# Grouped-query stage: four tiles projected abreast, sums and rotations dealt out anew, the last rotation cut into three steps

## The reference, cut to what matters

```python
def gqa_axial_mixer(hn, w_q, w_kv, q_gain, k_gain, w_o, cos_r, sin_r, cos_c, sin_c):
    q = (hn @ w_q).reshape(b, s, GQA_HEADS, GQA_HEAD_DIM).transpose(0, 2, 1, 3)      # 16 heads of 64
    kv = (hn @ w_kv).reshape(b, s, 2, GQA_KV_HEADS, GQA_HEAD_DIM)                    # 4 key/value heads
    k, v = kv[:, :, 0].transpose(0, 2, 1, 3), kv[:, :, 1].transpose(0, 2, 1, 3)
    q, k = rmsnorm(q, q_gain), rmsnorm(k, k_gain)                                    # over each head's 64
    def axial(t):
        return jnp.concatenate([apply_rope(t[..., :half], cos_r, sin_r),
                                apply_rope(t[..., half:], cos_c, sin_c)], axis=-1)
    o = blocked_attention(axial(q), axial(k), v, GQA_HEAD_DIM ** -0.5)
    return o.transpose(0, 2, 1, 3).reshape(b, s, GQA_HEADS * GQA_HEAD_DIM) @ w_o
```

## Time and profile before

| | |
|---|---|
| median of 3 runs | 1137.16 us (1133.55 to 1137.99) |
| the profiled execution | 1132.8 us, of which the profiler's span is 1130.9 us |
| PE busy | 1098.0 us, 97% of the span |
| DVE, ACT, POOL busy | 837.4, 619.0, 40.1 us |
| granted TensorE clock | 0.996 of full speed on average |
| the stage from its first matmul to its last output | 835.29 to 911.07 us of the span |

### The profile page before, as it was taken

One profiled execution on the slowest core, in us unless ns is written; L12 is line 12 of the kernel. 1 busy time (PEld: TensorE's weight loads), 2 busy tenths in 40 slices (PEclk: granted clock), 3 DMA queues, 4 the chain that ended last, 5 costly groups with the idle time before them and its releaser, 6 DMA issues.

```text
span 1130.9 us, 20116 instructions
## 1 busy us (share of the span) xinstructions
PE 1098.0 (97%) x7645; PEld 971.9 (86%) x7645; DVE 837.4 (74%) x1275; ACT 619.0 (55%) x1112; POOL 40.1 (4%) x42
## 2 busy tenths in 40 slices
PE   5999999999999999999999999999999899999997
PEld 5997779999899999999876889999988688888886
DVE  5698873665788878875467588788787867878875
ACT  6753446565545545573465555455465855545544
POOL 2000000010100000010000100000010001000000
PEclk9999999999999999999999999999999999999999
DMA  9551223343657657465320366656677055657651
GB/s 298 165 187 39 76 76 100 124 152 104 202 160 214 184 153 219 136 219 154 127 65 1 113 181 191 197 171 189 195 143 175 9 150 168 177 160 220 185 160 65
DMA packets 218591, 169.69 MB, mean 150 GB/s; under 512 B 20859, under 2 KB 208290, under 8 KB 218402
## 3 DMA queue, kind: packets, MB, share of 16 engines
q1 hardware_dynamic: 217106, 164.43, 49.6%
q0 software_dynamic: 912, 4.00, 1.1%
q10 hardware_dynamic: 512, 0.40, 0.1%
HBM read 167.76 MB, written 1.05 MB: 149 GB/s over the span
## 4 chain that ended last, share of the span: by engine, by line
PE 86%; DVE 5%; ACT 5%; SPq 1%; issue 1%; DMA 1%; POOLq 0%; POOL 0%; DVEq 0%; ACTq 0%
PE bank L2542 20%; PE bank L2161 18%; PE bank L2090 11%; PE bank L2092 10%; PE bank L2091 10%; PE bank L2544 10%; PE bank L2155 2%; PE bank L2156 2%; PE bank L2157 2%; DVE wlo L1427 1%; DVE arena L1420 1%; ACT arena L1370 1%; DVE wlo L1837 1%; SPq L702 1%; DMA arena<-in_ssm_lam_im_dram 1%
## 5 line engine op out<-in xcount | busy, mean ns | idle before, releaser
L2542 PE MATMUL bank<-mem_pair,whi 128*128 128x512 f32 x1056 | 375.8, 399 | 0.7 <-DVE xT L1758 0.7
L2544 PE MATMUL bank<-mem_pair,wlo 128*128 128x256 f32 x1056 | 296.7, 281 | 0.0
L2542 PEld LDWEIGHTS bank<-mem_pair,whi 128*128 128x128 f32 x1056 | 198.6, 188 | 47.5 <-issue 0.9
L2090 PE MATMUL bank<-act_hi,whi 128*128 128x256 f32 (+1 forms) x744 | 215.8, 290 | 2.3 <-DVE act_lo L1459 1.5
L1837 DVE TENSOR_TENSOR wlo<-raw,whi 128x1024 fp32r<-128x1024 f32 x177 | 208.9, 1221 | 5.3 <-ACT whi L1207 1.6
L2091 PE MATMUL bank<-act_lo,whi 128*128 128x256 f32 (+1 forms) x744 | 212.2, 285 | 0.0
L2092 PE MATMUL bank<-act_hi,wlo 128*128 128x256 f32 (+1 forms) x744 | 212.0, 285 | 0.0
L1427 DVE TENSOR_TENSOR wlo<-raw,whi 128x1024 fp32r<-128x1024 f32 (+3 forms) x137 | 162.0, 1224 | 65.6 <-ACT whi L783 64.5
L2544 PEld LDWEIGHTS bank<-mem_pair,wlo 128*128 128x128 f32 x1056 | 199.7, 189 | 0.8
L1207 ACT ACTIVATE whi<-raw 128x1024 fp32r<-128x1024 f32 x180 | 179.7, 1045 | 0.3 <-PE bank L2161 0.3
L1227 ACT ACTIVATE arena<-arena 128x256 f32<-128x256 f32 x66 | 27.6, 418 | 249.4 <-DVE arena L1420 249.4
(11 more groups left out here) (237 smaller groups left out, 1418.9 us busy)
## 6 DMA issues: line engine op xcount, KB each, us to landing
raw<-in_ffn_w_in_dram SPq DMA_DIRECT2D x132, 512.0 KB, 5.2
raw<-in_ffn_w_out_dram SPq DMA_DIRECT2D x33, 1024.0 KB, 5.0
raw<-in_w_in_ab_dram SPq DMA_DIRECT2D x11, 1024.0 KB, 6.2
raw<-in_w_in_dram SPq DMA_DIRECT2D x9, 1024.0 KB, 7.6
raw<-in_xa_wk_dram SPq DMA_DIRECT2D x4, 1024.0 KB, 5.4
raw<-in_xa_wv_dram SPq DMA_DIRECT2D x4, 1024.0 KB, 5.2
raw<-in_w_out_dram SPq DMA_DIRECT2D x4, 1024.0 KB, 5.0
raw<-in_xa_wq_dram SPq DMA_DIRECT2D x4, 1024.0 KB, 5.0
```

The lines of the kernel that those rows point to most:

```text
L2090: pe.matmul(dst, w[0], a[0], start=start, stop=False, **kw)
L2542: pe.matmul(b[:].rearrange("p (h t) -> p h t", h=2), w[0][:, k, g, :], mem_pair[:, :, k, :], start=k == 0, stop=False, skip_group_check=True)
L2544: last = pe.matmul(b[:, 0:T], w[1][:, k, g, :], mem_hi[:, k, :], start=False, stop=k == KC - 1, skip_group_check=True)
```

## The change

Three things change. First, gq0 and gq1 join the key tiles in `project_abreast`: four tiles abreast instead of two, and then gq2 to gq7 one by one. Second, the hooks are dealt out over six tiles instead of eight; gq2, gq4 and gq6 carry two each, the others one. The sum of squares of the stream goes to bank 7 instead of 5, since bank 5 now belongs to a tile in progress (gq2). Third, `g_rotate(4)` is cut into its three operations, at the ends of turns 2, 3 and 4 of the pair loop on DVE. PE's output of turn 4 needed the whole rotation because it writes bank 7; now it waits for the first step alone (`s_turn` 1), the one that reads this bank.

```diff
--- before.py
+++ after.py
@@ -477,7 +477,7 @@
         s_rq = sem("rotary_in"); s_rot = sem("rotary_swapped"); s_rd = sem("rotary_done")
         s_dscore = sem("dil_scores"); s_dbias = sem("dil_biased"); s_dmax = sem("dil_max"); s_dexp = sem("dil_exp")
         s_dp = sem("dil_probs"); s_dpt = sem("dil_transposed"); s_dpte = sem("dil_probsT"); s_do = sem("dil_out")
-        s_gain = sem("final_gain_landed"); s_fin = sem("final_sums_done")
+        s_turn = sem("last_rotation_step"); s_gain = sem("final_gain_landed"); s_fin = sem("final_sums_done")
         s_mean = sem("final_mean_square"); s_scale = sem("final_scale_ready"); s_fine = sem("final_evacuated")
         s_store = sem("stored")
 
@@ -814,7 +814,7 @@
 
             def x_rms_of(n):
 
-                k, ss = stat_no["norm", n], bank[5 if n == 6 else 4][:, 0:T]
+                k, ss = stat_no["norm", n], bank[7 if n == 6 else 4][:, 0:T]
                 act.wait_ge(s_xss, n - 1)
                 act.wait_ge(*stat_release(k - 2))
                 r = rms[:, k % 2, 0:T]
@@ -2047,6 +2047,7 @@
                     r = rsum[:, a:a + 2, :].rearrange("p h l -> p (h l)")
                     mul(pr, pr, r.unsqueeze(2).to_broadcast([P, 2 * TT, T])).then_inc(s_p, 2)
 
+                last_q = gqn[:, G_ORDER[4], :, :]
                 for i in range(pairs + 4):
                     if i == 1:
                         g_mean(4)
@@ -2061,7 +2062,13 @@
                     if 2 <= i <= pairs:
                         scale_pair(first + 2 * i - 2)
                     if i == 2:
-                        g_rotate(4)
+                        dve.wait_ge(s_rot, 10)
+                        mul(grot, bank7(P, 2), sin_g.unsqueeze(1).to_broadcast([P, 2, T])).then_inc(s_turn, 1)
+                    if i == 3:
+                        mul(last_q, last_q, cos_g.unsqueeze(1).to_broadcast([P, 2, T])).then_inc(s_turn, 1)
+                        dve.wait_ge(s_turn, 2)
+                    if i == 4:
+                        dve.tensor_tensor(last_q, last_q, grot, ALU.add).then_inc(s_rd, 1)
                     if i >= 4:
                         c = i - 4
                         dve.wait_ge(s_ohi, OHI[8 + c])
@@ -2182,7 +2189,7 @@
 
                 pe.wait_ge(s_acc, 4 * (n - 2) + 4)
                 pe.wait_ge(s_rms, 2 * stat_no["norm", n] - 1)
-                plain(bank[5 if n == 6 else 4][:, 0:T], ones[:], x_sum[:, 0:T]).then_inc(s_xss, 1)
+                plain(bank[7 if n == 6 else 4][:, 0:T], ones[:], x_sum[:, 0:T]).then_inc(s_xss, 1)
 
             def keep_clock(count, b=7):
 
@@ -2757,12 +2764,12 @@
             def g_sum(i):
                 sum_squares(("g", G_ORDER[i]), 0, bank[4][:], 2, True, True, blocks, claimed=i == 0)
 
-            project_abreast(6, [("gk", k, ("gkv", 0), P * k) for k in range(2)])
-            GQ_HOOKS = ({4: lambda: g_sum(0), 6: lambda: norm_sum(6)}, {4: lambda: x_rms_columns(6)},
-                        {4: lambda: g_sum(1)}, {4: lambda: g_swapped(0)},
-                        {4: lambda: g_sum(2)}, {4: lambda: g_swapped(1)},
-                        {4: lambda: g_sum(3)}, {4: lambda: g_swapped(2)})
-            for n in range(8):
+            project_abreast(6, [("gk", k, ("gkv", 0), P * k) for k in range(2)]
+                            + [("gq", k, ("gq", 0), P * k) for k in range(2)])
+            GQ_HOOKS = {2: {4: lambda: g_sum(0), 6: lambda: norm_sum(6)}, 3: {4: lambda: x_rms_columns(6)},
+                        4: {2: lambda: g_sum(1), 5: lambda: g_swapped(0)}, 5: {4: lambda: g_sum(2)},
+                        6: {2: lambda: g_swapped(1), 5: lambda: g_sum(3)}, 7: {4: lambda: g_swapped(2)}}
+            for n in range(2, 8):
                 project("gq", n, ("gq", n // 2), P * (n % 2), XN, hooks=GQ_HOOKS[n])
 
             def gqa_scores(tile, b):
@@ -2815,7 +2822,7 @@
                         a = first + 2 * c
                         pe.wait_ge(s_pte, a + 2)
                         if c == 1:
-                            pe.wait_ge(s_rd, 10)
+                            pe.wait_ge(s_turn, 1)
                         if c >= 2:
                             pe.wait_ge(s_olo, OHI[8 + c - 2])
                         gqa_values(c, bank[6 + c % 2], (gprobsT[:, a % 4, :, :], gprobsT[:, (a + 1) % 4, :, :]))
```

## The result

The changed kernel takes 1138.76 us, the median of 21 runs (lowest 1137.06); the kernel before takes 1134.0 us in 21 runs beside it (lowest 1132.25). The ratio is 1.0039, 95% interval 1.0028 to 1.0050, and the medians are 4.8 us apart. The forecast was 1140.8 us, in a range of 1136.0 to 1144.5, so the measured time is in the range. The forecast stood on a base of 1137.16 us and a difference of +3.6 us; the base has come down by 3.2 us with more runs, and the difference was 1.2 us too small.

A forecast was written before the change was run, and what follows sets the result against it. The prediction took PE, busy 97% of the span, to bound the kernel. A pair loop opening 4.6 us late less 1.0 us gained there made +3.6 us on 1137.16, so 1140.8 us, range 1136.0 to 1144.5.

The forecast's parts named there:

- Term 1: In the opening, four tiles abreast run without the waits for `x_low`: a gain of 1.6 us.
- Term 2: Ahead of gq2, PE waits 3.3 us for weights, the low parts of piece gq1, split late on ACT.
- Term 3: Ahead of gq4, PE waits 2.6 us for weights, whose split on ACT follows `norm_sum(6)`.
- Term 4: Behind gq4, three DVE chains of 5.87 us delay `scores(0)` to 0.6 us behind PE; pair loop opens 4.6 us late.
- Term 5: In the pair loop, ACT's exponentials of turn 3 start earlier with the rotation cut up: a gain of 1.0 us.
- Rival C: In the pair loop, the cut rotation gives nothing because maxima are delayed elsewhere: 1141.8 us, chance 0.12.
- The sum: Over the profiled execution, a pair loop opening 4.6 us late less 1.0 us gained in it: +3.6 us.
- rival A: In the waits ahead of gq2 and gq4, PE's clock falls, costing 2.4 us more: 1143.2 us, chance 0.27.
- Rival B: Ahead of gq2 and gq4, splits come early enough and all waits vanish: -3.0 us, 1134.2 us, chance 0.08.
- Its weaker form: Only the wait ahead of gq4 remains, gq2 starting at 846.9: 1137.5 us, chance 0.10.

The follow-up runs named there:

- third kernel: The changed kernel with ACT splitting piece gq1 ahead of the key tiles' squares instead of behind them: 1134.95 us, ratio 1.0002 to the kernel before.
- eighth kernel: The changed kernel with PE's two waits filled by 14 and 11 unread matmuls of ones: 1136.93 us, ratio 1.0032 to the kernel before.
- second kernel: The kernel before with only the last rotation cut into three steps: 1132.29 us, ratio 0.9984 to the kernel before.
- first kernel: The changed kernel with the whole last rotation put back in one block, keeping the new opening and hooks: 1139.03 us, ratio 1.0039 to the kernel before.
- fifth kernel: The changed kernel run once more, unchanged: 1138.53 us, ratio 1.0040 to the kernel before.
- fourth kernel: The changed kernel with the splits of gq1's and gq2's pieces both moved earlier on ACT and DVE: 1130.56 us, ratio 0.9970 to the kernel before.
- ninth kernel: The fourth kernel run once more, unchanged: 1134.45 us, ratio 0.9995 to the kernel before.
- sixth kernel: The changed kernel with PE's two waits filled by 26 and 20 unread matmuls of ones: 1144.41 us, ratio 1.0076 to the kernel before.

## Why the prediction was right, point by point

**Term 1** stood: no wait for `x_low` behind the first step, and 96 matmuls in 11.74 us (851.59 - 839.85), where 11.6 were predicted.

**Term 2** stood in its mechanism: 3.10 us ahead of gq2 on PE, released by the low parts, where 3.3 were predicted, and gq2 14.84 us into the stage, where 14.9 were. The third kernel shows the cause, since moving that split alone removes the wait. **Term 3** stood too: 2.44 us for 2.6, and moving the second split removes it. The third kernel's start of gq4, 21.94 us into the stage, is the same chain from an earlier gq2.

**Term 4** stood: `g_mean` at 870.97, 876.68 and 882.38, with DVE never idle between them, so 5.71 us a chain instead of 5.87, and `scores(0)` released by `g_scaled(3)`, though with 0.22 us of wait for 0.6. Without a fall of the clock they come 42.37 us into the stage (eighth kernel), where 42.7 were predicted.

**Term 5** was right in its mechanism and a little large: 0.84 us in after and 0.82 in the second kernel, for 1.0; ACT's wait became one for PE, of 0.38 us for 0.5. Rival C, nothing from the loop, is out.

**The sum** of the five, +3.6, is what the eighth kernel gives (+3.41 in the stage, +3.4 in the median): the opening costs 42.37 - 38.13 = 4.24 us, for 4.6, and the loop gives 0.83 back, for 1.0.

What failed is the choice between this case and **rival A**, the clock. The prediction gave 0.43 to no fall and 0.27 to the fall, and it named a clock below 1 behind these waits as a sign that the forecast is wrong. That sign came. Four profiles have these waits unfilled, seven waits in all, and the clock fell in or behind six of them: both in after, both in the first kernel, the only one in the third, and the first in the fifth, but not the second there, of 2.44 us. In the two kernels with the waits filled it fell at none. The price of a fall was mis-sized: 2.4 us were taken from the row at 25.2 us. Here `norm_sum(6)` comes 4.71 us behind the start of gq2 with the fall (fifth kernel) and 854.19 - 851.09 = 3.10 us without (eighth), so one fall delays it by 1.6 us, and nearly all of that reaches the end of the stage: 4.98 - 3.41 = 1.57. Where it stays down for longer behind the first wait and falls behind the second as well, as in the profile of after, the stage is 83.14 us, another 2.4 longer. The Trainium skill, "TensorE: Matmul & The Clock Gate", section "HAM oscillation — how this bites in real kernels", says that a wait in mid-kernel can send the clock back to its lower level; the rows above agree, and the forecast should have leaned on it and on the earlier trace rows more than on the waits of 1.3 us.

So the forecast of 1140.8 lies 2.0 us above the measured 1138.76 by two errors of opposite sign: the difference was 1.2 us too small (1.4 for the fall left out, less the 0.2 by which the other terms together were too large), and the base was the median of 3 runs, two of them from the upper group, 3.2 us above that of 21. That the number came so close is in part luck. On the base of 21 runs the same sum gives 1134.0 + 3.6 = 1137.6 us and rival A 1134.0 + 6.0 = 1140.0, and the measured 1138.76 lies about halfway between them.

**Rival B** did not happen to this change, but the fourth kernel is it: both waits gone, -2.63 us in the stage, where -3.0 were worked out. The condition that the prediction named, a split of gq1 that ends 3.2 us earlier, was only a matter of ACT's order. Its weaker form, the second wait alone, is the third kernel: +1.37 us in the stage, with a fall of the clock in it, against +0.3 worked out without one. Less the 1.57 us of one fall it would be -0.2, an estimate that no run here tests.

## What to carry to other kernels

Moving work of the bounding engine forward takes the cover from whatever was prepared behind that work: look in the other engines' queues for the first thing that the moved work now needs, and ask whether it stands there behind something that waits for the moved work itself. Here two splits stood behind operations that had become later, and putting them where ACT was idle anyway turned a loss of 4.98 us in the stage into a gain of 2.63. Waits like these two (3.10 and 2.44 us on TensorE) should be priced with a slow stretch of the clock behind them, since six of the seven here had one, and a median of a few runs shouldn't be the base of a forecast finer than the distance between the kernel's groups of times.

## What the runs showed of the hardware that was not expected

- The granted clock fell at waits of 3.10 and of 2.44 us (third kernel: 1.00 until 859, 0.50 from 860 to 862, 1.00 again from 863), but stayed at 1.00 at the second wait of the fifth kernel, also of 2.44 us. It fell some 1.3 us after work had resumed in the fifth kernel, but already in the wait in the profile of after. The slow stretch lasted some 3 us in the fifth kernel and some 7 us behind the first wait of after. What decides this stayed open.
- The two groups of times go with one more such fall, far ahead of the stage. Windows from 99 to 109 us, of after and then of the ninth kernel:

```profile
99.00:109.00 10.00, 10.00 (x32) 7.37 (x32) 6.86 (x11) 4.54 (x10) 0.00 (x0) 0.51 0.01 2
```

```profile
99.00:109.00 10.00, 10.00 (x68) 8.53 (x67) 8.67 (x13) 5.41 (x12) 0.00 (x0) 1.00 0.01 2
```

  32 matmuls instead of 68 in 10 us. The stage starts at 839.60 to 839.99 us in the three profiles with the fall (after, second and fourth kernel), and at 835.27 to 836.33 in the eight without it. In both of the profiles shown PE had an idle gap some 3 us ahead of that, ending at 96.3 us: 1.50 us in after, 1.20 in the ninth; but the fourth has the fall with one of 0.87 us. So the length of that one gap doesn't decide it, and the cause wasn't found.
- An fp32 matmul of 128x128 with 128 columns took 0.22 us in a row of its like (sixth kernel), nearly twice the 0.12 us of the reduced-precision ones with 256 columns (96 in 11.74 us in after).
